# Attention's values held twice side by side: one product of 128 columns by 512 in place of two of 64 by 256

## What is computed

```python
def swa_sink_attention(h, w_qkv, w_o, q_gain, k_gain, sinks):
    q, k, v = jnp.split(h @ w_qkv, [A_Q_COLS, A_Q_COLS + A_KV_COLS], axis=-1)
    q, k = rotary(rmsnorm(q, q_gain)), rotary(rmsnorm(k, k_gain))     # 16 query heads, 2 key/value heads, width 64
    ...                                                               # 8 chunks of 64; a chunk sees itself and the one before
    scores = jnp.einsum('bnqhgd,bnkhd->bnhgqk', qb, kb) * (A_HEAD_DIM ** -0.5)
    m = jnp.maximum(jnp.max(scores, axis=-1, keepdims=True), sink)
    p = jnp.exp(scores - m)
    probs = p / (jnp.sum(p, axis=-1, keepdims=True) + jnp.exp(sink - m))
    out = jnp.einsum('bnhgqk,bnkhd->bnqhgd', probs, vb)
    return out.reshape(B, S, A_Q_COLS) @ w_o
```

## Time and profile before

| | |
|---|---|
| time, median of 3 runs | 1265.23 us (1265.06 to 1265.63) |
| the profiled execution | 1265.3 us, of which the profiled span is 1263.1 us |
| PE busy | 1258.7 us (100% of the span) |
| PE weight loads | 1041.6 us (82%), beside the products |
| DVE busy | 714.2 us (57%) |
| ACT busy | 465.0 us (37%) |
| POOL busy | 141.1 us (11%) |
| chain that ended last | PE 99%, DVE 1% |

### The profile page before, as it was taken

One profiled execution on the slowest core, in us unless ns is written; L12 is line 12 of the kernel. 1 busy time (PEld: TensorE's weight loads), 2 busy tenths in 40 slices (PEclk: granted clock), 3 DMA queues, 4 the chain that ended last, 5 costly groups with the idle time before them and its releaser, 6 DMA issues.

```text
span 1263.1 us, 15562 instructions
## 1 busy us (share of the span) xinstructions
PE 1258.7 (100%) x5856; PEld 1041.6 (82%) x5856; DVE 714.2 (57%) x907; ACT 465.0 (37%) x655; POOL 141.1 (11%) x138
## 2 busy tenths in 40 slices
PE   9999999999999999999999999999999999999999
PEld 8777888888888888888888888888888888888887
DVE  6786586666664333545545634644686667663222
ACT  6664454444442222232233223223454444442120
POOL 3751300000000010412103101201000000000000
PEclk9999999999999999999999999999999999999999
DMA  7212222222222224322212222221232222222322
GB/s 245 68 34 99 77 100 100 100 100 100 100 68 92 92 91 161 120 85 91 100 67 75 100 100 75 100 79 55 100 109 100 100 98 87 87 78 97 105 91 89
DMA packets 21909, 120.43 MB, mean 95 GB/s; under 512 B 2552, under 2 KB 3856, under 8 KB 11120
## 3 DMA queue, kind: packets, MB, share of 16 engines
q1 hardware_dynamic: 20928, 117.61, 26.9%
q10 hardware_dynamic: 720, 1.97, 0.4%
q0 software_dynamic: 224, 0.35, 0.1%
HBM read 117.81 MB, written 2.11 MB: 95 GB/s over the span
## 4 chain that ended last, share of the span: by engine, by line
PE 99%; DVE 1%; POOL 0%; issue 0%; DVEq 0%
PE ps L1307 32%; PE ps L1309 31%; PE ps L1308 31%; PE ps L1351 1%; PE ps L1448 1%; PE ps L1435 1%; PE ps L1426 1%; PE ps L1324 0%; DVE w_lo L666 0%; PE ps L1345 0%; PE ps L1409 0%; DVE mx L767 0%; POOL qs L1200 0%; DVE qss L739 0%; PE ps L1337 0%; PE ps L1399 0%
## 5 line engine op out<-in xcount | busy, mean ns | idle before, releaser
L1307 PE MATMUL ps<-h_hi,w_hi 128*128 128x512 f32 x960 | 375.3, 391 | 0.0
L1309 PE MATMUL ps<-h_hi,w_lo 128*128 128x512 f32 x960 | 373.6, 389 | 0.0
L1308 PE MATMUL ps<-h_lo,w_hi 128*128 128x512 f32 x960 | 373.5, 389 | 0.0
L666 DVE TENSOR_TENSOR w_lo<-raw,w_hi 128x2048 fp32r<-128x2048 f32 (+1 forms) x115 | 244.4, 2125 | 141.0 <-ACT w_hi L352 141.0
L352 ACT ACTIVATE w_hi<-raw 128x2048 fp32r<-128x2048 f32 (+1 forms) x115 | 202.6, 1762 | 211.7 <-PE ps L1309 211.7
L1309 PEld LDWEIGHTS ps<-h_hi,w_lo 128*128 128x128 f32 x960 | 180.2, 188 | 37.6
L1307 PEld LDWEIGHTS ps<-h_hi,w_hi 128*128 128x128 f32 x960 | 180.3, 188 | 37.5
L1308 PEld LDWEIGHTS ps<-h_lo,w_hi 128*128 128x128 f32 x960 | 180.3, 188 | 36.6
L1307 PE MATMUL ps<-g_hi,w_hi 128*128 128x512 f32 x352 | 136.9, 389 | 0.0
L1308 PE MATMUL ps<-g_lo,w_hi 128*128 128x512 f32 x352 | 136.9, 389 | 0.0
L1309 PE MATMUL ps<-g_hi,w_lo 128*128 128x512 f32 x352 | 136.9, 389 | 0.0
(11 more groups left out here) (170 smaller groups left out, 1440.6 us busy)
## 6 DMA issues: line engine op xcount, KB each, us to landing
raw<-in_w_up SPq DMA_DIRECT2D x44, 1024.0 KB, 4.8
raw<-in_w_ret SPq DMA_DIRECT2D x32, 1024.0 KB, 4.8
raw<-in_w_dn SPq DMA_DIRECT2D x32, 704.0 KB, 4.0
raw<-in_w_ao SPq DMA_DIRECT2D x4, 1024.0 KB, 4.9
raw<-in_w_q SPq DMA_DIRECT2D x3, 1024.0 KB, 5.1
gain_x<-in_xT SPq DMA_DIRECT2D x7, 256.0 KB, 4.8
out<-gain_x SPq DMA_DIRECT2D x7, 256.0 KB, 5.2
rbc<-root_mem SPq DMA_DIRECT2D x6, 256.0 KB, 3.1
```

What stands on the lines that cost most here:

```text
L666: nc.vector.tensor_tensor(w_lo[:, s, 0:cols], raw[:, s, 0:cols], w_hi[:, s, 0:cols].bitcast(F32), ALU.subtract).then_inc(w_lo_ok, 1)
L1307: nc.tensor.matmul(dst, st[0], mv[0], start=start, stop=False)
L1308: nc.tensor.matmul(dst, st[0], mv[1], start=False, stop=False)
L1309: return nc.tensor.matmul(dst, st[1], mv[0], start=False, stop=stop)
```

## The change

`va` and `ve` hold each key/value head's 64 columns twice, side by side, so a head has 128 columns. ACT's copy into `va` reads its source twice for that, and the two copies of POOL into `ve` become twice as wide. `values(g)` is one product of 128 held columns by all 512 columns of `pT`. It fills the whole bank: the even heads' results that are wanted stand in partitions 0 to 63, columns 0 to 255, and the odd heads' in partitions 64 to 127, columns 256 to 511; the other two quarters are not read. `heads_out(g)` takes the two quarters one after the other, each as 64 partitions by 256, with a high and a low part each; `alo_ok` is raised after the last of the four. `ahi_ok` counts two for a group.

```diff
-        va = sb("va", [P, PT, A_KVH * A_DH], scope=att)
-        ve = sb("ve", [P, PT, A_KVH * A_DH], scope=att)
+        va = sb("va", [P, PT, A_KVH * 2 * A_DH], scope=att)
+        ve = sb("ve", [P, PT, A_KVH * 2 * A_DH], scope=att)
...
-                nc.scalar.activation(va[:, t, :], ps[:, t, P:2 * P], ACT.Copy,
+                nc.scalar.activation(va[:, t, :].rearrange("p (c i d) -> p c i d", i=2, d=A_DH),
+                                     ps[:, t, P:2 * P].rearrange("p (c d) -> p c d", d=A_DH).unsqueeze(2)
+                                     .to_broadcast([P, A_KVH, 2, A_DH]), ACT.Copy,
                                      scale=rcol[:, 0, t:t + 1]).then_inc(v_ok, 1)
...
-                src = ps[:, PV_BANK, 0:4 * CHUNK].rearrange("p (j q) -> p j q", q=CHUNK)
-                dst = (slice(None), slice(4 * c, 4 * c + 4), slice(n * CHUNK, (n + 1) * CHUNK))
                 dve.wait_ge(pv_done, g + 1)
-                nc.vector.tensor_copy(a_hi[dst], src).then_inc(ahi_ok, 1)
-                dve.wait_ge(ahi_ok, g + 1)
-                nc.vector.tensor_tensor(a_lo[dst], src, a_hi[dst].bitcast(F32), ALU.subtract).then_inc(alo_ok, 1)
+                for par in range(2):
+                    rows = slice(par * A_DH, (par + 1) * A_DH)
+                    src = ps[rows, PV_BANK, par * 256:(par + 1) * 256].rearrange("p (j q) -> p j q", q=CHUNK)
+                    dst = (rows, slice(4 * c, 4 * c + 4), slice(n * CHUNK, (n + 1) * CHUNK))
+                    nc.vector.tensor_copy(a_hi[dst], src).then_inc(ahi_ok, 1)
+                    dve.wait_ge(ahi_ok, 2 * g + par + 1)
+                    low = nc.vector.tensor_tensor(a_lo[dst], src, a_hi[dst].bitcast(F32), ALU.subtract)
+                low.then_inc(alo_ok, 1)
...
-                for par in range(2):
-                    last = nc.tensor.matmul(ps[par * A_DH:(par + 1) * A_DH, PV_BANK, 0:4 * CHUNK],
-                                            v[:, n // 2, c * A_DH:(c + 1) * A_DH],
-                                            pT[:, g % 2, par * 256:(par + 1) * 256], start=True, stop=True)
-                last.then_inc(pv_done, 1)
+                nc.tensor.matmul(ps[:, PV_BANK, :],
+                                 v[:, n // 2, c * P:(c + 1) * P],
+                                 pT[:, g % 2, :], start=True, stop=True).then_inc(pv_done, 1)
```

## The result

The changed kernel takes **1276.74 us** (1276.55 to 1276.90, 4 runs) against 1265.39 (1265.06 to 1265.63) for the kernel before in the same runs: 11.35 us or 0.9% slower, ratio 1.0089 with a 95% interval of 1.0077 to 1.0101. The direction was forecast; the size was not. The forecast was +7.6, and the time lies above its range.

What follows compares the result with a forecast made beforehand. PE was taken as the bound, in step with DVE. PE's own 3.4 us plus 4.2 us of waits for DVE made +7.6 us, 1272.8 us forecast; own range 1271.3 to 1274.8, with rivals 1268.7 to 1274.8.

Steps and rivals of the forecast that it cites:

- The product, 0.87 us, and +3.4 us for PE: values(g) on PE: new product 0.87 us against 0.79; +0.7 us over 7 groups, +2.7 over 9 beside scores or starting fresh.
- The factor of up to 2 for products side by side: Skill rule against the change: 64-column tiles run in parallel; by it alone values' products double, 10.4 us more on PE.
- 0.80 us a group on DVE: heads_out's second high and low pair costs DVE 0.80 us a group, 12.8 in all; ends 0.37 and 0.85.
- The six places, +4.0: PE waits for DVE at values(1), turn(3), values(4), values(8), values(9) and the output projection's second half: 0.4 to 0.8 us each.
- PE's growth covers 0.7 us of DVE's: At PE's waits for DVE, PE's own lateness was taken to cover 0.7 us of DVE's added lateness.
- Rival C: values(g): new product costs no more than the old pair, 0.79 or less; DVE's waits grow to 4.9; 1270.1 us, chance 0.06.
- At the other groups the pair costs nothing: Groups 5, 6, 7, 10 to 14: PE has 0.7 us or more of other work between, so nothing is lost.
- rival B: At PE's waits, DVE's lateness is absorbed by PE's own growth; only 3.4 us is left, 1268.7 us; chance 0.05.
- The copies are hidden: ACT's and POOL's wider copies, and the queries' rotation behind POOL's, cost nothing; without that cover up to 1 us.
- A: heads_out on DVE: half-high instructions are cheaper, 0.37 us extra a group in place of 0.80; 1270.2 us, chance 0.10.
- D: values(g) on PE: product at 0.46 us in place of 0.79, -5.3 us; 1260.0 us at best, chance 0.03.
- E: Whole kernel: no change that can be seen, from combined rivals; 1264.2 to 1267.5 or 1267.6 us, chance 0.04.

Runs made afterwards that it cites:

- pe_only: Kernel before with only values(g) made one product of 128 by 512 columns, narrow va and ve, heads_out as before; 1268.56 us, +3.2.
- padded: Kernel before with zeros beside each head's values and values(g) as two accumulating full-array products of 128 by 256, heads_out untouched; 1268.85 us, +3.3.
- rep_low: Kernel before plus a second DVE pair per group, of partitions 0 to 63, into a tile nobody reads; 1270.37 us, +5.0.
- rep_full: Kernel before plus a second DVE pair per group, of all 128 partitions, into a tile nobody reads; 1270.53 us, +5.2.
- after_low: Changed kernel, but heads_out is one 128-partition pair plus an unread pair of partitions 0 to 63; 1274.56 us, +9.0 against the kernel before.
- rep_high: Kernel before plus a second DVE pair per group, of partitions 64 to 127, into a tile nobody reads; 1272.84 us, +7.5.
- pe_copies: Changed kernel with heads_out as before, one pair of 128 partitions by 256; 1269.02 us, +3.7 against the kernel before.
- va_only: Kernel before with only va and ACT's copies into it doubled, ve and POOL's copies narrow; 1265.41 us, -0.2.
- dve_split: Kernel before with heads_out in two halves of 64 partitions, both from columns 0 to 255; products and copies as before; 1273.01 us, +7.7.
- copies_only: Kernel before with va, ve and the ACT and POOL copies doubled, products and DVE as before; 1265.98 us, +0.7.

## Why the prediction was wrong in size

- *PE is the bound, and PE and DVE run in step.* Right. Beside PE's own growth, the losses stand where PE's timeline has waits.
- *The product, 0.87 us, and +3.4 us for PE.* Right: 0.85 us, +3.2 us (`pe_only`), and with `padded` +3.3. The broadcast of 1024 columns in the full array was the right row to read it from, and the pause of 0.10 us at a change between whole and divided array was rightly kept on scores' side and taken away on the other.
- *The factor of up to 2 for products side by side, from the Trainium skill, "TensorEngine Tiling (Array Packing)", Overview.* The rows show 1.5: the four records of 256 columns take 0.58 us from their start to the next one's when they run side by side (47.29 to 47.88 in the kernel before is 0.59), and 0.85 in the full array (`padded`). With the two pauses of 0.10 that go away the products cost +3.2, not the +10.4 of the factor alone.
- *A half-high instruction costs what a full one does.* Right, `rep_low` against `rep_full`. The row on POOL led to the right answer on DVE.
- *0.80 us a group on DVE.* **This term failed.** It took the step to the next instruction from rows in which every instruction starts at partition 0 and begins while the one ahead still runs. The second pair starts at partition 64, and what follows at 0 again; both begin only when the one ahead has ended. It measured 0.96 to 0.98 (1.0 against the typical 0.80), and this is worth 2.2 us (changed kernel against `after_low`) to 2.5 (`rep_high` against `rep_low`). For a second pair that also starts at partition 0 the 0.80 was right: 0.74 to 0.78. The range's upper end of 0.85 rested on the same rows.
- *The six places, +4.0.* Right for the pair that was priced. The table under this list tells what DVE's second pair costs PE's timeline at the forecast's six places, and what elsewhere.
- *PE's growth covers 0.7 us of DVE's.* Not borne out. Rival C had put DVE alone at 4.9, and `rep_low` measured 5.0, but that the two meet is luck: C had the 4.9 at the six places, the trace has 4.1 there and 0.9 elsewhere. With PE's growth the six places lose 4.1 as well. Growth does cover 0.2 us at `turn(3)`, and it costs as much more at the second half of the projection.
- *At the other groups the pair costs nothing.* **This step failed too**, by 1.3 us without the change of partition and by 2.3 with it. `values(11)`, 12, 13 and 15 start 0.98, 0.87, 0.98 and 0.98 us behind the end of a_lo in the kernel before; PE needs 0.15 of that: where it waits for a_lo, it starts 0.14 to 0.15 behind its end. The 0.83 that is left at three of them holds a pair of 0.78, and `rep_low` loses under 0.05 at each of these three. But PE's growth shrinks the slack instead of opening it: in `pe_copies` the four distances are 0.74, 0.81, 0.74 and 0.75. The longer product hands its bank to DVE later by 0.36 us, while PE comes to the next `values` later by only 0.12 (rows under the list). The argument against rival B said it: what waits on PE's end moves with PE. The sum did not heed it. A product that has to wait also takes 0.08 us more (0.93 against 0.85).
- *The copies are hidden.* ACT's are (`va_only`), POOL's are not: 0.7 us. The question asked was whether `ve` is there in time; the rotation behind the copies, and beside which of DVE's instructions it then runs, was passed over with a sentence. That it might come to 1 us uncovered had been said, and it was counted in the upper end only.

`values(10)`, `heads_out(10)` and `values(11)` in the kernel before:

```profile
96.52 0.65 PE L1448 MATMUL ps<-rbc,ve 128*64 128x256 f32 x4
97.22 0.43 DVE L789 CAST a_hi<-ps 128x256 fp32r<-128x256 f32 x1 [0.94 <-PE ps L1448]
99.08 0.65 PE L1448 MATMUL ps<-rbc,va 128*64 128x256 f32 x4
```

and in `pe_copies`:

```profile
99.53 1.02 PE L1449 MATMUL ps<-rbc,ve 128*128 128x512 f32 x2
100.59 0.42 DVE L791 CAST a_hi<-ps 128x256 fp32r<-128x256 f32 x1 [1.31 <-PE ps L1449]
102.21 1.02 PE L1449 MATMUL ps<-rbc,va 128*128 128x512 f32 x2
```

From the product's start to a_hi it is 0.70 us, and 1.06 in `pe_copies`; from one product's start to the next it is 2.56, and 2.68 there. Such a wait of DVE for PE stands in the trace ahead of 6 of the 16 `heads_out` before, and of 7 in the changed kernel.

| us that DVE's second pair adds, by PE's starts | six places | elsewhere | sum |
|---|---|---|---|
| forecast, pair of 0.80 | 3.95 | 0.2 | 4.2 |
| `rep_low` against the kernel before | 4.1 | 0.9 | 4.9 |
| `after_low` against `pe_copies` | 4.1 | 1.5 | 5.6 |
| `dve_split` against the kernel before | 5.3 | 2.0 | 7.3 |
| changed kernel against `pe_copies` | 5.2 | 2.5 | 7.6 |

A line is read so: the lateness of one kernel's PE behind the other's is taken at the product that follows each `values(g)`, and what it grows by from one such point to the next is put down to the place between them. Each line compares two single profiled executions, from `values(0)` to 128 us in the time of the kernel before, and is read from starts that are rounded to 0.01; the sums agree with the medians' differences (5.0, 5.3, 7.7 and 7.65) within 0.4.

What was measured in place of the sum: 3.2 for PE, 0.7 for the copies, 5.0 for DVE's second pair, 2.5 for its start partition: 11.4. The rivals fall: A by `rep_low` against `rep_full`, B by `pe_copies`, which lacks 7.7 us of the changed kernel's loss, C by `pe_only` with its +3.2, D by the 0.85 us in the row, and E by the result itself.

## What to carry to other kernels

Price an added instruction by the step to its neighbours, not by its duration, and read that step from rows where the neighbours stand as they will: on DVE going from partition 0 to 64 cost the overlap of the two instructions, and so did coming back. Where two engines hand work to and fro, don't count the growth of one as cover for the other: a product that ends later hands over later, and takes slack from the engine behind it. Of work that is hidden, ask what is queued behind it and what that will then run beside.

## What the runs showed of the hardware

- DVE: an instruction of 64 partitions by 256 takes 0.38 to 0.43 us, mostly 0.42 or 0.43, and so does one of 128. Behind a low part at partition 0, an instruction at partition 0 that has nothing to wait for begins after 0.34 to 0.35 us (`rep_low`, `rep_full`), one at partition 64 after 0.43 to 0.44, and one at 0 behind a low part at 64 after 0.45 to 0.46 (`rep_high`).
- PE, float32: 128 columns by 512 take 0.85 us in the full array, as two products of 256 that add up or as one; 0.93 where they had waited for DVE and their weight loads began only 0.03 us ahead. Two products of 64 columns by 256 side by side took 0.58 to 0.61 from their start to the next one's, with a pause of 0.10 at each end where the array is used whole next to them.
- A DVE step of 2048 columns took 2.28 us, and 2.56 when POOL's rotation ran on beside its beginning (`copies_only` and `va_only`; by what means is open).
